# LRU depthwise convolution as diagonal-weight matmuls on TensorE, interleaved with the gates

## The reference, cut to what matters

```python
xc = depthwise_conv(lru_x, lru_conv_w, lru_conv_b, 2)        # 4 taps along time, per channel
r = sigmoid(blockdiag(xc, w_a) + b_a);  i = sigmoid(blockdiag(xc, w_x) + b_x)
log_a = -8 * r * softplus(-lam);        a = exp(log_a)
u = sqrt(-expm1(2 * log_a)) * (i * xc)  # needs a*a = exp(2 log_a)
h = scan(a, u)                          # forward; a second set of weights runs backward
y_lru = gelu(lru_g) * (h_forward + h_backward)
```

## Time and profile before

| | before |
|---|---|
| time, median of 3 runs | 2692.57 us (lowest 2692.39) |
| the profiled execution | 2692.75 us, its slowest core's span 2691.1 us |
| spans of the 8 cores | 2673.4 to 2691.1 us |
| busy share of the span: PE, DVE, ACT, POOL | 72%, 54%, 50%, 10% |
| matmul instructions of PE | 9056 |
| chain that ended last, by engine | PE 36%, ACT 24%, DVE 18%, issue 12%, DMA 6% |

### The profile page before, as it was taken

How to read it: one execution, slowest core, us unless ns; L and a number is a source line. 1 busy time by engine, 2 the same in 40 slices (tenths; PEclk the granted TensorE clock), 3 DMA queues, 4 the chain that set the end, 5 groups by cost and what they waited for, 6 DMA issues and landing times.

```text
span 2691.1 us, 27100 instructions; the slowest of 8 cores (2673.4 to 2691.1 us)
## 1 busy us (share of the span) xinstructions
PE 1949.6 (72%) x9056; PEld 814.6 (30%) x9056; DVE 1454.0 (54%) x1347; ACT 1357.5 (50%) x1578; POOL 280.7 (10%) x468
## 2 busy tenths in 40 slices
PE   4732378888567888879957323888875688888897
PEld 2410132222233333334434101222222233333343
DVE  2568744343464777742335687434344656777423
ACT  4668578888133333321155795787872333333211
POOL 1101210000401111110011112000013011111000
PEclk9875699999798999989978656999997899999899
DMA  6400000000247333363343000000003563333332
GB/s 163 81 0 4 20 1 8 8 1 1 73 155 94 34 34 32 32 100 113 110 138 68 2 12 10 1 16 1 1 1 92 154 79 33 35 36 32 82 110 102
DMA packets 128567, 139.11 MB, mean 52 GB/s; under 512 B 95792, under 2 KB 96304, under 8 KB 128304
## 3 DMA queue, kind: packets, MB, share of 16 engines
q0 software_dynamic: 103616, 47.07, 14.6%
q1 hardware_dynamic: 24816, 90.31, 10.6%
HBM read 148.76 MB, written 33.55 MB: 68 GB/s over the span
## 4 chain that ended last, share of the span: by engine, by line
PE 36%; ACT 24%; DVE 18%; issue 12%; DMA 6%; POOL 2%; SPq 0%; ACTq 0%; DVEq 0%; POOLq 0%
PE ps L426 34%; ACT sb L394 22%; DVE sb L408 14%; DMA sb<-out 3%; POOL sb L397 2%; PE ps L429 2%; DVE sb L397 2%; ACT L394 1%; DMA sb<-x 1%; ACT sb L412 1%; DVE sb L436 1%; DMA sb<-w_up 1%; DMA sb<-w_down 1%; DVE sb L432 1%; SPq L374 0%
## 5 line engine op out<-in xcount | busy, mean ns | idle before, releaser
L426 PE MATMUL ps<-sb 128*128 128x512 bf16 (+3 forms) x8160 | 1878.0, 381 | 508.2 <-ACT sb L394 275.9
L426 PEld LDWEIGHTS ps<-sb 128*128 128x128 bf16 (+1 forms) x8160 | 752.7, 99 | 1606.7 <-issue 894.2
L394 ACT ACTIVATE sb<-sb 128x1024 f32<-128x1024 f32 (+9 forms) x424 | 373.9, 891 | 720.8 <-DVE sb L408 373.5
L408 DVE SCALAR_TENSOR_TENSOR sb<-ps,sb 128x2047 f32<-128x2047 f32 (+1 forms) x304 | 506.5, 1674 | 238.9 <-ACT sb L394 219.5
L394 ACT ACTIVATE sb<-ps 128x1024 bf16<-128x1024 f32 (+1 forms) x544 | 516.7, 996 | 124.3 <-PE ps L426 123.9
L423 DVE RECIPROCAL sb<-ps 64x1024 f32<-64x1024 f32 x32 | 209.9, 6559 | 384.8 <-PE ps L426 384.8
L394 ACT ACTIVATE sb<-ps,sb 128x2048 f32<-128x2048 f32 (+1 forms) x152 | 246.3, 1655 | 168.6 <-PE ps L426 168.4
L397 POOL TENSOR_TENSOR sb<-sb 128x512 bf16<-128x512 bf16 (+4 forms) x272 | 157.1, 601 | 1225.0 <-PE ps L426 696.7
L408 DVE SCALAR_TENSOR_TENSOR sb<-sb 128x1024 bf16<-128x1024 f32 (+3 forms) x224 | 256.3, 1176 | 11.8 <-DVE sb L423 0.9
L429 PE MATMUL ps<-sb 128*128 128x128 bf16 (+1 forms) x896 | 80.8, 244 | 219.2 <-DVE sb L408 108.1
L397 DVE TENSOR_TENSOR sb<-ps,sb 128x128 f32<-128x128 f32 (+2 forms) x256 | 127.7, 551 | 203.9 <-DMA sb<-out 126.8
(11 more groups left out here) (18 smaller groups left out, 149.7 us busy)
## 6 DMA issues: line engine op xcount, KB each, us to landing
sb<-x SPq DMA_DIRECT2D x64, 512.0 KB, 5.3
out<-sb SPq DMA_DIRECT2D x64, 512.0 KB, 3.3
sb<-w_up POOLq DMA_DIRECT2D x88, 256.0 KB, 4.4
sb<-out SPq DMA_DIRECT2D x32, 512.0 KB, 4.3
sb<-w_down POOLq DMA_DIRECT2D x44, 256.0 KB, 10.1
sb<-w_in POOLq DMA_DIRECT2D x16, 360.0 KB, 18.7
sb<-w_o POOLq DMA_DIRECT2D x16, 256.0 KB, 22.0
sb<-cst SPq DMA_DIRECT2D x6, 512.0 KB, 4.5
```

Of the source, the lines that this page charges most:

```text
L394: P.add("act", lambda e: e.activation(out=o, in_=i, func=func, **kw), reads=rd, writes=wr)
L408: P.add("dve", lambda e: e.scalar_tensor_tensor(out=o, in0=a, scalar=s, in1=b, op0=op0, op1=op1), reads=rd, writes=[o])
L426: P.add("pe", lambda e: e.matmul(o, l, r, start=start, stop=stop), reads=[l, r], writes=[o])
```

## The change

The four taps become matmuls. For each chunk and tap a 128x128 float32 matrix is built that has the tap's weights on its diagonal (16 matrices, 8 built by DVE and 8 by POOL, at the start of M3). `lru_conv_mm(c)` issues 16 matmuls, 4 output tiles of 512 by 4 taps, all with float32 operands, into PSUM banks 0 to 3; `lru_conv_evac(c)` brings the four banks to `xc` with one Identity on ACT, which adds the bias, and DVE makes the bf16 copy. In chunk c the matmuls of chunk c+1 stand behind the Tanh of the first pair, and the evacuation behind that pair's Sqrt.

Two more things change in the same diff: `a2` is no longer an Exp of its own on ACT but the square of `ra`, taken by DVE; and the fourth buffer set is made in chunk 1 and no longer in chunk 0, since `xl0` and `xl1`, whose space it takes, are released later. So chunk 0 has three sets: its first pair takes sets 0 and 1, its second sets 2 and 0, and the first pair of chunk 1 again 0 and 1.

```diff
+            diagws = [alloc(f"diagw{i}", F32, [8, 128]) for i in range(2)]
+            diag_ap = lambda ck: diagws[ck // 8][:, ck % 8, :]
+            for ck in range(16):
+                ts("pool" if ck % 2 else "dve", diag_ap(ck), CST[:, C_IDENT:C_IDENT + 128], CST[:, C_CW + ck:C_CW + ck + 1], None, ALU.mult)
+            def lru_conv_mm(c):
+                for t in range(4):
+                    for k in range(4):
+                        mm(psb(t), diag_ap(c * 4 + k), xl[c][:, k + t * 512:k + (t + 1) * 512], k == 0, k == 3)
-            def lru_conv(c):
+            def lru_conv_evac(c):
                 xc_ = xcs[c % 2]
-                cw = lambda k: CST[:, C_CW + c * 4 + k:C_CW + c * 4 + k + 1]
-                act(xc_, xl[c][:, 0:T], AF.Identity, bias=CST[:, C_CB + c:C_CB + c + 1], scale=cw(0))
-                for k in range(1, 4):
-                    stt(xc_, xl[c][:, k:k + T], cw(k), xc_, ALU.mult, ALU.add)
+                act(xc_.rearrange("p (a b) -> p a b", a=4), PS[:, 0:4, :], AF.Identity, bias=CST[:, C_CB + c:C_CB + c + 1])
                 cp("dve", xcbs[c % 2], xc_)
                 A.release(f"xl{c}")
-            lru_conv(0)
+            lru_conv_mm(0)
+            lru_conv_evac(0)
...
-                if c + 1 < 4:
-                    lru_conv(c + 1)
-                if c == 0:
+                if c == 1:
                     sets.append((alloc("ra3", F32, [HT]), alloc("a23", F32, [HT]), alloc("iu3", F32, [HT])))
-                for pair in (((0, 0), (1, 1)), ((0, 1), (1, 0))):
+                for pi, pair in enumerate((((0, 0), (1, 1)), ((0, 1), (1, 0)))):
...
+                    if pi == 0 and c + 1 < 4:
+                        lru_conv_mm(c + 1)
                     for it, (d, hf) in enumerate(pair):
...
-                        act(a2_, ra_, AF.Exp, bias=COEF1[:, col:col + 1], scale=COEF1[:, col:col + 1])
                         act(ra_, ra_, AF.Exp, bias=COEFH[:, col:col + 1], scale=COEFH[:, col:col + 1])
+                        tt("dve", a2_, ra_, ra_, ALU.mult)
...
                         act(a2_, a2_, AF.Sqrt, bias=QTR, scale=-0.25)
+                    if pi == 0 and c + 1 < 4:
+                        lru_conv_evac(c + 1)
```

More of the change, by code:

```diff
@@ L710, in build_program @@
                 stt(yTl[:, c, :], h0, CST[:, C_GGRP + c:C_GGRP + c + 1], gg[:, c, :], ALU.mult, ALU.mult)
-            for nm in ("xc0", "xc1", "xcb0", "xcb1", "ra0", "a20", "iu0", "ra1", "a21", "iu1", "ra2", "a22", "iu2", "ra3", "a23", "iu3", "h0", "h1b", "gg", "gate_b"):
+            for nm in ("diagw0", "diagw1", "xc0", "xc1", "xcb0", "xcb1", "ra0", "a20", "iu0", "ra1", "a21", "iu1", "ra2", "a22", "iu2", "ra3", "a23", "iu3", "h0", "h1b", "gg", "gate_b"):
                 A.release(nm)
```

## The result

The changed kernel takes 2774.72 us (median of 9 runs) against 2693.14 us; the ratio is 1.0314, with a 95% interval of 1.0282 to 1.0346. It is slower. The profiled execution took 2771.01 us, its slowest core's span is 2769.5 us.

What follows compares the result with a forecast made beforehand. No engine is full: M3 loops through ACT, DVE and POOL waiting in turn. The walk through M3 summed 11.5 + 12.8 + 2.3 + 10.2 + 3.4 = +40.2 us a sequence, giving 2773 us; range 2745 to 2815.

Steps and rivals of the forecast that it cites:

- The place and the worth of a microsecond: M3, run twice, is the only stage touched; its end passes on in full to the program's end, twice.
- The float32 matmul: On PE in M3: four passes at the high clock, 0.884 us each, against 0.221 us for bf16.
- rival of half the passes: Rival for M3's bursts: C = 8.6 us, +14.6 us a sequence, 2722 us, within 2%; chance 0.09.
- The burst: PE's 16 matmuls for a chunk: 16 x 0.884 + 2 for low clock = 16.1 us; bounds 3.5 and 28.3.
- The start: M3's beginning: burst, evacuation, cast and gates put the first Tanh at 182.8 instead of 171.29, +11.5 us.
- Chunk 0: M3's first chunk: DVE waits for the burst, next Tanh for the shared set; 46.6 us against 33.85, +12.8.
- Chunks 1 and 2: M3's middle chunks: next Tanh at 37.9 us, +2.3 and +10.2; DVE, backlogged to T+12.1, waits 5.3 us for PE.
- Chunk 3: M3's last chunk, without a burst: 43.9 us against 40.5, +3.4, as squares stand in DVE's queue.
- The sum: M3's five excesses: +40.2 us a sequence, +80.4 for both; 2773 us, 3.0% slower.
- DVE is all that counts: Rival: DVE runs M3 without a gap, end at 295.0, -13.9 us a sequence, 2665 us; chance 0.04.
- a burst of up to 10.8 us hides in chunks 1 and 2: In M3's chunks 1 and 2, bursts up to 10.8 us are hidden; each microsecond above is paid.
- the clock might stay low: Rival for M3's bursts: clock stays 1.2 GHz, C = 28.3, +89 us, 2871; chance 0.19 shared with unhidden weight loads.

Runs made afterwards that it cites:

- the kernel with four sets: The changed kernel with the fourth buffer set from chunk 0 on and only chunk 0's four matrices built: 2748.57 us, ratio 1.0198.
- two taps: The changed kernel without taps 2 and 3, so 8 float32 matmuls a burst instead of 16: 2741.92 us, ratio 1.0158.
- the bf16 burst: The changed kernel with bf16 xl and diagonal matrices, so the convolution's matmuls are bf16: 2730.72 us, ratio 1.015.
- squares alone: The kernel before, with only the second Exp on ACT replaced by a square on DVE: 2720.81 us, ratio 1.009.
- bf16 and the queues set in order: The changed kernel with bf16 convolution, early chunk 0 burst, four sets, cast moved later, both Exp on ACT, POOL idle in chunks: 2670.38 us, ratio 0.9915.
- the best version with the taps on DVE: The kernel before, with both iu operations ahead of a pair's scans and POOL's products given to DVE: profiled execution 2678.9 us.

## Why the prediction was right, point by point

- **The place and the worth of a microsecond.** Right: 75.3 of 78.3 us lie in the two runs of M3.
- **The float32 matmul.** Right in size: 0.874 us at full clock against 0.884, reached as two records of two passes' time each. The rival of half the passes falls. The Trainium skill's page "Perfetto Trace Analysis", section "Engine Utilization", has half the rate for FP32_LOW_HIGH; by the timeline each record ran at half the rate of bf16 (0.437 us against 0.221), but a matmul is two records, so it ran at a quarter. With four passes, as the Trainium skill's page "FP8 and Floating Point Precision", section "TensorE Precision Notes", has it, the trace agrees. That a load is twice as dear as a bf16 one I had not foreseen; it stayed hidden, 0.437 us a record at full clock.
- **The burst.** 15.8, 14.0, 16.4 and 16.2 us against 16.1 for each. The 2 us for the low clock are right for three; chunk 0's burst started at full clock.
- **The start.** First Tanh at 181.55, predicted 182.8; M3 itself began 0.4 us earlier than before, the burst was 0.3 us shorter.
- **Chunk 0.** 44.55 us against 46.6; the burst was 2.1 us shorter. Its wait for the shared set, 9.00 us, was predicted at 8.7 (46.6 against 37.9), and the kernel with four sets shows that some 8 us of it are paid.
- **Chunks 1 and 2.** 37.9 and 37.7 us against 37.9. DVE's wait ahead of the cast in chunk 2 is 4.93 (predicted 5.3), in chunk 0 9.69 (11.1). In chunk 1 it is 12.09, where I had said 5.3. This is the step that was wrong: I let chunk 1 begin with DVE's backlog reaching to T+12.1, but the shared set had just held up its Tanh by 8.7 us, and the backlog was gone at T+3.4. It cost the sum nothing, since PE's burst set the end of that wait either way. It did cost the rival "half the passes", and so did a second step: the walk took all of DVE's wait in chunk 2 as the price of the burst. But the evacuation also stands behind the pair's Sqrt on ACT, and that Sqrt behind squares which wait for DVE's leftover work. By the walk's own times (squares done at 14.4) the Sqrt end at about 17, just ahead of the burst. The trace has T+17.1 for the Sqrt and T+17.5 for the burst, and the evacuation waited for PE 0.43 us, where it was 5.19 in chunk 0 and 7.59 in chunk 1. With two taps the chunks shortened by just that, 5.3, 7.6 and 0.5 us, and the start by 6.8: 20.3 us, where the prediction priced a shorter burst at 7.5, 7.5, 5.3 and 5.3, together 25.6. So the length of chunk 2 came out right because two chains end almost together there; the burst alone does not make it.
- **Chunk 3.** 44.3 us (301.71 to 346.00) against 43.9; the squares' wait in DVE's queue is what it has over the 40.5 before.
- **The sum.** +80.4 predicted, +78.3 measured in the profiled executions; M3 189 against 186.2 us. The small errors at the start and in chunk 0 have one sign, and 3 us outside M3, which I had put at nothing, the other.
- **A slip in a rival.** "DVE is all that counts" has 9.2 us for the squares of a sequence. There are 16, at 2.3 us for two 18.4 us, as in the 4.6 us a chunk further up. With that its M3 ends at 304.2, 4.7 us earlier than before, and the time is 2683 us, not 2665. Neither occurred: with the bf16 burst M3 lasted 13.5 us longer than before.
- **What was only argued.** That a burst of up to 10.8 us hides in chunks 1 and 2. The traces put the edge where the burst ends with the Sqrt. With two taps they ended at T+10.07 and T+10.15 in chunk 1, so a burst of about 8.9 us is hidden there; in chunk 2 of the changed kernel it would be about 15.9. Both are estimates from these rows, as no burst between 9 and 14 us was run. That the clock might stay low: in the changed kernel's rows the bursts of the start and of chunk 1 were at full clock after some 3 to 5 us.

## What to carry to other kernels

In float32 the depthwise convolution on TensorE did not pay: a matmul of 512 columns cost 0.87 us against 0.22 in bf16, and the burst took longer than the 7.3 us of DVE work that it replaced. With bf16 alone it did not pay either (+1.5%); it did with bf16 and the queues set in order, and then by little: M3 lasted 135.3 us where the best version with the taps on DVE has 139.5. Before moving work to an idle engine, look at what stands behind the handover in each in-order queue: of 37.5 us lost a sequence, 12.6 came back by moving one cast of 1.2 us behind work that was ready, and 8.4 by a fourth buffer set. An operation moved from one engine to another can lengthen a loop in which neither is full (squares alone: +13 us a sequence), since the length is that of the round trip. And before taking a wait away, look for the engine that will set the pace then: of 20.8 us of waits for POOL 8.0 came back, because ACT had next to no idle time left.

## What the runs showed of the hardware that I had not expected

- A float32 matmul of the program runs as two instructions on PE, each with a weight load of its own; at full clock each took 0.437 us for 512 columns, and a load 0.21 us (mean) where bf16 has 0.10.
- A POOL product of two 1024-element float32 operands beside DVE's scans cost DVE 1.9 us a pair of scans (6.43 us together in place of 4.6), and with POOL's squares added DVE's add of 2048 elements went from 2.29 to 3.37 us. With POOL idle the scans were at 2.31 us. M3 gained only 1.3 us a sequence when POOL's product went away, since DVE did not set its pace.
- The granted clock was 0.50 over the first 3.3 us of the first burst and the first 4.2 us of the one in chunk 1, and 1.00 in the rows that begin 3.8 and 5.1 us into them. After 6.8 us in which PE did 1.9 us of gate matmuls it was still 1.00.
